# Four pairs of units by seven block products in each feed-forward phase instead of three

## The chip, the core and the metric

One NeuronCore of a Trainium2 chip runs the whole program. The metric is the device time in microseconds of one execution, from the runs of the same program.

## What is computed

A trunk of four layers over 256 tokens of width 1024. Each layer is a feed-forward block, an attention block (stick-breaking, differential, forgetting or again stick-breaking) and a second feed-forward block, each added to x, and at the end comes a norm. The change touches the feed-forward blocks alone, of which there are eight:

```python
D, F = 1024, 2816
def swiglu(x, w_gate, w_up, w_down):
    return (jax.nn.silu(x @ w_gate) * (x @ w_up)) @ w_down
...
x = x + 0.5 * swiglu(rms_norm(x, norm_g[i, 0]), ffn_w_gate[i, 0], ffn_w_up[i, 0], ffn_w_down[i, 0])
```

## The kernel before

**Precision.** Every product is made of three: each operand is split into a rounded part (hi, type fp32r) and the rest (lo = value - hi), and `product` adds hi*hi, hi*lo and lo*hi into PSUM. So each weight chunk (1 MB, 128x2048) is loaded into a slot of `raw`, turned into `w_hi` on ScalarE (`hi`, L462) and into `w_lo` on VectorE (`lo`, L750), and only then is it used by TensorE. `w_hi` and `w_lo` are rings of six chunks (`RING`), so chunk c may be split only when chunk c - 6 has been used (`slot_free`).

**Units.** The 2816 columns of gate and up are 11 units of 256 (`UNITS`). A plain unit has two chunks, `top` and `bottom` (the two halves of the contraction, gate and up side by side), each multiplied with both blocks of 128 tokens; that is 4 x 12 = 48 matmuls of 512 columns. Then silu and the product with up (`silu` on ScalarE, `gated` on VectorE), four transposes on TensorE (`hidden`), a split of the result (`hidden_hi`, `hidden_lo`) and the unit's `down` chunk, 24 matmuls into the four accumulating banks `acc`.

**Pairs.** Two neighbouring units can be made together by a scheme of seven block products instead of eight (token block by half of the contraction, on one side; half of the contraction by unit, on the other). The four weight blocks are b11, b12, b21, b22; VectorE forms four sums of them (`form`: t1, t2, t3, t4, each 128x2048), of which b12 itself isn't used. The seven parts used by TensorE are b11, t1, t2, b21, t3, t4, b22 (`PARTS`), each a split chunk of its own and a `quarter` of 12 matmuls. The results in PSUM are put together by copies on ScalarE (`copied`), sums on VectorE (`summed`), `pair_silu` and `hidden_of`. The sums of the tokens that the scheme needs are made once in each phase (`token_sums_hi`, `token_sums_lo`). `SEVEN` = 2, 5, 8 are the units at which a pair begins; units 0, 1, 4, 7, 10 are plain. So a phase has 5 x 2 + 3 x 7 + 11 = 42 split chunks and 33 loads.

**Order.** All orders are written by hand. `FFN_ORDER` sets the order of the chunks, which ScalarE and VectorE walk with `split_to(c)` (split all up to chunk c, in order), with the other work put between. `plan` gives each load a slot and the event that frees it: four slots of `raw` in turn, and two of `extra`, one for the result of t1 and t4 (`SUMS`), one for b22 (`EXTRA`). The SyncE queue issues the loads in order, each behind the wait for its slot. The engines run their lists in order and meet at semaphores; TensorE waits for `lo_ready` before each chunk, VectorE for `hi_ready`, ScalarE for the load or the form, and for the ring.

In the trace L1259, L1260 and L1261 are the three matmuls of `product`; L1461 is `hidden` (4 transposes), L1417 `pair_hidden` (8 for a pair); L750 the split on VectorE, L763, L766, L770, L774 the forms t1, t3, t2, t4; L814 `hidden_lo`, L844 `token_sums_lo`, L903 `summed`, L848 `gated`, L854 and L918 the products with up in a pair; on ScalarE L462 is the split, L485 `hidden_hi`, L530 `copied`, L496, L534 and L548 the silus; L1172 is the update of x that ends a phase.

## Time and profile before

| | us |
|---|---|
| median of 3 runs (1890.7 to 1891.03) | 1890.84 |
| the profiled execution, its own time | 1890.51 |
| its span | 1888.3 |
| busy in the span: TensorE | 1874.2 (99%) |
| VectorE | 1532.0 (81%) |
| ScalarE | 1073.1 (57%) |

The span is what the profiler records between the first and the last instruction; 2.2 us lie around it. The busy time of TensorE counts each matmul to its modelled end, so that neighbours overlap: what counts is the distance from one start to the next. The busy time of a VectorE instruction is likewise a little longer than the distance to the next one.

### The profile page before, as it was taken

The numbers are of one execution on the slowest core, as the hardware profiler recorded it, in microseconds if no ns is written. First come the engines' busy times: TensorE is split into PE (matmuls) and PEld (weight loads), VectorE is DVE, ScalarE is ACT, GpSimd is POOL, SyncE is SP. The second block draws the span as 40 slices with busy tenths as digits, with TensorE's granted clock in tenths as the row PEclk, the third lists the DMA queues.
The fourth block names the chain that finished last, engine by engine and source line by source line (L and its number), as shares of the span: only waits on it lengthen the run. The fifth ranks groups of instructions, "written<-read, shape, count | busy, mean of one in ns | idle before, by whom it ended". The sixth has DMA issues, their size and how long they took to land.

```text
span 1888.3 us, 22487 instructions
## 1 busy us (share of the span) xinstructions
PE 1874.2 (99%) x9380; PEld 1586.9 (84%) x9380; DVE 1532.0 (81%) x1312; ACT 1073.1 (57%) x1107; POOL 19.9 (1%) x34
## 2 busy tenths in 40 slices
PE   9999999999999999999999999999999999999998
PEld 7888998888888898788888889988888888998886
DVE  7987568987898778898789875689879987559985
ACT  6655555655565544565566554466555654556653
POOL 0000000000000000100000000000000000000000
PEclk9999999999999999999999999999999999999999
DMA  6556343446254642454625454435463544533552
GB/s 249 201 231 267 135 157 134 201 201 244 94 226 198 240 159 109 156 201 200 256 103 226 197 221 157 175 116 201 200 267 122 227 196 191 183 130 137 228 196 86
DMA packets 50052, 350.13 MB, mean 185 GB/s; under 512 B 6168, under 2 KB 6432, under 8 KB 7968
## 3 DMA queue, kind: packets, MB, share of 16 engines
q1 hardware_dynamic: 49360, 346.54, 47.6%
q10 hardware_dynamic: 592, 2.17, 0.3%
q8 instruction: 74, 1.21, 0.3%
q14 instruction: 26, 0.21, 0.0%
HBM read 347.63 MB, written 1.06 MB: 185 GB/s over the span
## 4 chain that ended last, share of the span: by engine, by line
PE 89%; DVE 7%; ACT 2%; issue 1%; DMA 0%; POOL 0%; POOLq 0%; ACTq 0%; DVEq 0%
PE work L1259 18%; PE work L1261 18%; PE work L1260 18%; PE acc L1259 10%; PE acc L1261 10%; PE acc L1260 10%; DVE w_lo L750 3%; PE work L1417 1%; PE acc L1303 1%; PE work L1461 1%; PE work L1586 1%; ACT w_hi L462 1%; PE work L1552 0%; DMA x<-x_dram 0%; PE work L1556 0%
## 5 line engine op out<-in xcount | busy, mean ns | idle before, releaser
L750 DVE TENSOR_TENSOR w_lo<-raw,w_hi 128x2048 fp32r<-128x2048 f32 x327 | 741.3, 2283 | 33.6 <-ACT w_hi L462 33.5
L462 ACT ACTIVATE w_hi<-raw 128x2048 fp32r<-128x2048 f32 x327 | 613.9, 1909 | 83.3 <-DVE raw L770 63.2
L1259 PE MATMUL work<-w_hi,xg 128*128 128x512 f32 x1040 | 411.2, 395 | 1.0 <-DVE xg L1184 1.0
L1261 PE MATMUL work<-w_hi,xg 128*128 128x512 f32 x1040 | 405.6, 390 | 0.0
L1260 PE MATMUL work<-w_lo,xg 128*128 128x512 f32 x1040 | 404.9, 389 | 0.0
L1259 PE MATMUL acc<-w_hi,m_hi 128*128 128x512 f32 x824 | 325.6, 395 | 0.2
L1261 PE MATMUL acc<-w_hi,m_lo 128*128 128x512 f32 x824 | 321.2, 390 | 0.0
L1260 PE MATMUL acc<-w_lo,m_hi 128*128 128x512 f32 x824 | 320.9, 389 | 0.0
L1261 PEld LDWEIGHTS work<-w_hi,xg 128*128 128x128 f32 x1040 | 195.3, 188 | 41.5
L1259 PEld LDWEIGHTS work<-w_hi,xg 128*128 128x128 f32 x1040 | 195.3, 188 | 39.5 <-issue 1.2
L1260 PEld LDWEIGHTS work<-w_lo,xg 128*128 128x128 f32 x1040 | 195.5, 188 | 38.3
L1261 PEld LDWEIGHTS acc<-w_hi,m_lo 128*128 128x128 f32 x824 | 154.7, 188 | 32.7
L1259 PEld LDWEIGHTS acc<-w_hi,m_hi 128*128 128x128 f32 x824 | 154.8, 188 | 31.7 <-DVE w_lo L750 1.0
L1260 PEld LDWEIGHTS acc<-w_lo,m_hi 128*128 128x128 f32 x824 | 154.9, 188 | 30.7
L750 DVE TENSOR_TENSOR w_lo<-extra,w_hi 128x2048 fp32r<-128x2048 f32 x72 | 164.2, 2280 | 0.0
L462 ACT ACTIVATE w_hi<-extra 128x2048 fp32r<-128x2048 f32 x72 | 135.3, 1913 | 45.8 <-DVE extra L763 36.6
L1261 PE MATMUL work<-w_hi,wide_r 128*128 128x512 f32 x384 | 149.8, 390 | 0.0
L1259 PE MATMUL work<-xg,w_hi 128*128 128x256 f32 x512 | 148.7, 290 | 0.6 <-DVE fg L963 0.5
L1261 PE MATMUL work<-xg,w_lo 128*128 128x256 f32 x512 | 144.7, 283 | 0.0
L1260 PE MATMUL work<-xg,w_hi 128*128 128x256 f32 x512 | 144.7, 283 | 0.0
L485 ACT ACTIVATE m_hi<-work 128x512 fp32r<-128x512 f32 x88 | 49.9, 595 | 136.5 <-PE work L1417 109.8
L814 DVE TENSOR_TENSOR m_lo<-work,m_hi 128x512 fp32r<-128x512 f32 x88 | 58.3, 684 | 67.5 <-ACT m_hi L485 67.5
(199 smaller groups left out, 2175.4 us busy)
## 6 DMA issues: line engine op xcount, KB each, us to landing
raw<-stream_dram SPq DMA_DIRECT2D x303, 1024.0 KB, 5.0
extra<-stream_dram SPq DMA_DIRECT2D x24, 1024.0 KB, 6.9
x<-x_dram SPq DMA_DIRECT2D x2, 512.0 KB, 7.9
raw<-stream_dram ACTq DMA_DIRECT2D x2, 512.0 KB, 7.5
scratch<-cum_rows ACTq DMA_DIRECT2D x1, 1024.0 KB, 6.6
cst<-consts_dram SPq DMA_DIRECT2D x1, 832.0 KB, 6.4
out_dram<-x SPq DMA_DIRECT2D x3, 256.0 KB, 2.4
final_gain<-final_gain_dram SPq DMA_DIRECT2D x1, 512.0 KB, 6.7
```

Of the source, the lines that this page charges most:

```text
L462: nc.scalar.activation(w_hi[:, c % RING, :], raw_at(place), ACT.Copy).then_inc(hi_ready, 1)
L485: nc.scalar.activation(m_hi[:, u % 2 * 2:u % 2 * 2 + 2, :], halves(hidden_bank(s)), ACT.Copy).then_inc(h_hi_ready, 1)
L750: nc.vector.tensor_tensor(w_lo[:, c % RING, :], raw_at(place), w_hi[:, c % RING, :].bitcast(F32), ALU.subtract).then_inc(lo_ready, 1)
L814: nc.vector.tensor_tensor(m_lo[:, u % 2 * 2:u % 2 * 2 + 2, :], halves(hidden_bank(s)), m_hi[:, u % 2 * 2:u % 2 * 2 + 2, :].bitcast(F32), A ...
L1259: nc.tensor.matmul(dst, a_hi, b_hi, start=start, stop=False, skip_group_check=skip)
L1260: nc.tensor.matmul(dst, a_hi, b_lo, start=False, stop=False, skip_group_check=skip)
L1261: return nc.tensor.matmul(dst, a_lo, b_hi, start=False, stop=stop, skip_group_check=skip)
L1303: ins = nc.tensor.transpose(turned(bank)[:, d, :], x_part(bank)[:, d * P:(d + 1) * P], ident)
L1417: ins = nc.tensor.transpose(hidden_bank(s)[:, t * T + tb * P:t * T + (tb + 1) * P], h[:, t * P:(t + 1) * P], ident)
L1461: ins = nc.tensor.transpose(hidden_bank(s)[:, t * T + tb * P:t * T + (tb + 1) * P], hidden_source(s)[tb][:, t * P:(t + 1) * P], ident)
L1586: nc.tensor.matmul(bank, v[:, 0, cols], w[:, 0:T], start=True, stop=True)
```

## The change

- `SEVEN` = 3, 5, 7, 9: four pairs. Plain are units 0, 1, 2. The three plain units come first, then the four pairs one behind the other; before, plain units and pairs took turns. A phase has 3 x 2 + 4 x 7 + 11 = 45 split chunks, still 33 loads.
- The forms are made in place: t1 in the slot of b12, t2 over t1, t3 over b11, t4 over b21. So the two slots of `extra` become slots for loads, for the four blocks of a pair and for what is loaded between pairs (`plan`).
- The parts of a pair have three orders: `FIRST_PAIR` for unit 3, `NEXT_PAIR` for 5 and 7, `LAST_PAIR` for 9, with the `down` of earlier units between them. The end of a pair (last silu, last product with up, transposes) lies within the next one.
- The PSUM banks that the pairs use change from pair to pair (`ROLES`), and the intermediate tiles too (`pair_tiles`, a new tile `odd_parts`).
- VectorE splits one chunk of the next phase less ahead of the phase's end. `DMA_SCRATCH` goes from 8192 to 2048.

```diff
 UNITS = FF // COLS
-SEVEN = 2, 5, 8
+SEVEN = 3, 5, 7, 9
...
 RAW = 4
-DMA_SCRATCH = 8192
+ROLES = {s: ((3, 2, 1, 0), (1, 0, 3, 2))[i % 2] for i, s in enumerate(SEVEN)}
+DMA_SCRATCH = 2048
 RING = 6
...
-FORMS = "t1", "t3", "t2", "t4"
+FORMS = "t1", "t2", "t3", "t4"
 PARTS = "b11", "t1", "t2", "b21", "t3", "t4", "b22"
-PAIR_ORDER = *PARTS[:5], "down", *PARTS[5:]
+FIRST_PAIR = "b11", "t1", "t2", "b21", "t3", "b22", "down", "t4"
+NEXT_PAIR = "b11", "t1", "t2", "t3", "b22", "b21", "down", "down_next", "t4"
+LAST_PAIR = "b11", "t1", "t2", "t3", "b21", "down", "t4", "b22"
...
 def ffn_order():
     order = []
-    for s in range(UNITS):
-        if s in SEVEN:
-            order += [(what, s - (what == "down")) for what in PAIR_ORDER]
-        elif s - 1 in SEVEN:
-            continue
-        elif s - 2 in SEVEN:
-            order += [("top", s), ("bottom", s), ("down", s - 2), ("down", s - 1)]
-        else:
-            order += [("top", s), ("bottom", s)] + [("down", s - 1)] * (s > 0)
-    return order + [("down", UNITS - 1)]
+    for s in PLAIN:
+        order += [("top", s), ("bottom", s)] + [("down", s - 1)] * (s > 0)
+    downs = PLAIN[-1]
+    for s in SEVEN:
+        for what in pair_order(s):
+            if what in PARTS:
+                order.append((what, s))
+            else:
+                order.append(("down", downs))
+                downs += 1
+    return order + [("down", s) for s in range(downs, UNITS)]
...
-SUMS, EXTRA = RAW, RAW + 1
+SLOTS = RAW + 2
...
+
+    def load(what, layer, n, j, slots, until, release):
+        place = min(slots, key=lambda i: freed[i][0])
+        filled[place] += 1
+        loads.append((what, layer, n % 3, j, place, freed[place][1]))
+        freed[place] = until, release
+        return place, filled[place]
...
+        if not att:
+            freed[RAW:] = [(c0 + 2, ("top", no * len(PLAIN) + 1))] * 2
...
-                uses.append((what, no, j, *places["b12"]))
+            if what == "b11":
+                c = {part: c0 + order.index((part, j)) for part in PARTS}
+                last_form = len(FORMS) * (no * len(SEVEN) + SEVEN.index(j) + 1)
+                homes = {part: load(part, layer, n, j, range(SLOTS), until, release) for part, until, release in (
+                    ("b11", c["t3"], ("lo", c["t3"] + 1)), ("b12", c["b21"] + 1.5, ("form", last_form)),
+                    ("b22", c["b22"], ("lo", c["b22"] + 1)), ("b21", c["t4"], ("lo", c["t4"] + 1)))}
+            if what in PARTS:
+                home = homes[{"t1": "b12", "t2": "b12", "t3": "b11", "t4": "b21"}.get(what, what)]
...
-                              ("lo", c0 + order.index(("b22", SEVEN[earlier])) + 1)))
+                mixed = not att and ("b11", SEVEN[0]) in order[:w - c0] and j < SEVEN[-1]
+                home = load(what, layer, n, j, range(SLOTS if mixed else RAW), w, ("lo", w + 1))
...
-                    copied(1, 1, first_part)
+                    def last_silu(s):
+                        act.wait_ge(part_psum, len(PARTS) * (f * len(SEVEN) + SEVEN.index(s)) + part_number(s, "t4"))
+                        nc.scalar.activation(pair_tiles(SEVEN.index(s))[3], work[:, ROLES[s][0], 0:COLS], ACT.Silu,
+                                             scale=r_col[:, 1:2]).then_inc(pair_silu_ready, 1)
+
...
+                    split_to(q + 2)
+                    last_silu(SEVEN[SEVEN.index(s) - 1])
+                    split_to(q + 3)
+                    copied(1, u_bank, first_part)
+                    split_to(q + (5 if s < SEVEN[-1] else 4))
+                    copied(3, u_bank, first_sum)
+                    hidden_hi(s - 2)
                     hidden_hi(s - 1)
-                    split_to(q + 5)
...
+                    copied(2, w_bank, second_part)
+                    if s < SEVEN[-1]:
+                        split_to(q + 7)
+                        pair_silu(2, second_part, 1)
+                        pair_silu(3, first_sum, 0)
+                        split_to(q + 8)
+                        pair_silu(1, first_part, 0)
+                        split_to(q + 10)
+                        return
...
+
                 if what == "t1":
-                    if j == SEVEN[0]:
-                        dve.wait_ge(top_used, no * len(PLAIN) + 1)
-                    dve.wait_ge(raw_loaded[place["t3"]], 16 * USES[q + PAIR_ORDER.index("t3")][4])
-                    ins = nc.vector.tensor_tensor(raw_at(SUMS), b12, b11, ALU.subtract)
+                    loaded("b11")
+                    loaded("t1")
+                    ins = nc.vector.tensor_tensor(t1, t1, b11, ALU.subtract)
+                elif what == "t2":
+                    loaded("b22")
+                    dve.wait_ge(lo_ready, at["t1"] + 1)
+                    ins = nc.vector.tensor_tensor(t1, b22, t1, ALU.subtract)
...
-                    ins = nc.vector.tensor_tensor(b11, b12, b11, ALU.add)
+                    dve.wait_ge(form_ready, formed)
+                    dve.wait_ge(lo_ready, at["b11"] + 1)
+                    ins = nc.vector.tensor_tensor(b11, t1, b11, ALU.subtract)
...
-                    ins = nc.vector.tensor_tensor(raw_at(SUMS), b21, b11, ALU.subtract)
+                    dve.wait_ge(form_ready, formed)
+                    dve.wait_ge(lo_ready, at["b21"] + 1)
+                    ins = nc.vector.tensor_tensor(b21, b21, t1, ALU.subtract)
...
                         hidden_lo(0)
                         token_sums_lo((2,))
+                        split_to(c0 + 7)
+                        gated(1, 0)
+                        gated(1, 1)
+                        q = c0 + FFN_ORDER.index(("b11", s + 2))
                         form("t1", q)
-                    else:
-                        form("t1", q)
-                        split_to(q)
+                        split_to(q + 1)
+                        form("t2", q)
+                        form("t3", q)
+                        return
+                    q = c0 + FFN_ORDER.index(("b11", s + 1))
+                    hidden_lo(1)
+                    split_to(q + 2)
+                    gated(s, 0)
+                    split_to(q + 3)
+                    gated(s, 1)
+                    form("t4", q)
+                    split_to(q + 4)
+
...
+                        return
+                    if s > SEVEN[1]:
+                        form("t3", q)
+                    split_to(q + 2)
+                    last_hidden(SEVEN[SEVEN.index(s) - 1])
+                    if s < SEVEN[-1]:
+                        split_to(q + 5)
                         hidden_lo(s - 2)
                         hidden_lo(s - 1)
-                    form("t3", q)
-                    form("t2", q)
-                    gated(s, 0)
-                    gated(s, 1)
+                        form("t4", q)
+                        summed(2, second_part, "t3", u_bank)
+                        split_to(q + 6)
+                        hidden_of(s, 2, second_part, 1)
+                        summed(3, first_sum, "b22", w_bank)
+                        split_to(q + 7)
+                        hidden_of(s, 3, first_sum, 0)
+                        summed(1, first_part, "b21", z_bank)
+                        form("t1", q + 9)
+                        split_to(q + 8)
+                        hidden_of(s, 1, first_part, 0)
+                        split_to(q + 10)
+                        form("t2", q + 9)
+                        return
...
-                split_to(c0 + FFN_CHUNKS + 2)
+                split_to(c0 + FFN_CHUNKS + 1)
...
-                    quarter(1, block_of(1, 1), q + 6, False, True)
+                    quarter(u_bank, sum_of(S2), at("t2"), False, False)
                     if s == SEVEN[0]:
+                        quarter(z_bank, block_of(0, 1), at("b21"), True, True)
+                        pe.wait_ge(part_copied, 3 * p + 2)
+                        quarter(u_bank, sum_of(S3), at("t3"), False, False)
+                        pe.wait_ge(part_copied, 3 * p + 3)
                         pe.wait_ge(token_lo_ready, BANKS * (f + 1))
-                    quarter(3, sum_of(S4), q + 7, False, True)
+                        quarter(w_bank, sum_of(S4), at("b22"), False, True)
+                        unit_down(s - 1).then_inc(down_used, 1)
+                    else:
+                        pair_hidden(p - 1, s - 2)
+                        pair_hidden(p - 1, s - 1)
+                        pe.wait_ge(part_copied, 3 * p + 2)
+                        quarter(u_bank, sum_of(S3), at("t3"), False, False)
+                        if s < SEVEN[-1]:
+                            pe.wait_ge(part_copied, 3 * p + 3)
+                            quarter(w_bank, sum_of(S4), at("b22"), False, True)
+                        pe.wait_ge(h_split, f * UNITS + s - 1)
+                        quarter(z_bank, block_of(0, 1), at("b21"), True, True)
+                        unit_down(s - 2).then_inc(down_used, 1)
+                        if s < SEVEN[-1]:
+                            unit_down(s - 1).then_inc(down_used, 1)
+                    pe.wait_ge(pair_sums_ready, 3 * p + sum_number(s, 2))
+                    quarter(u_bank, block_of(1, 1), at("t4"), False, True)
```

On VectorE, before: from the first form of the pair of units 5 and 6 to its fourth form.

```order
L763 TENSOR_TENSOR extra<-raw 128x2048
L750 TENSOR_TENSOR w_lo<-raw,w_hi 128x2048
L814 TENSOR_TENSOR m_lo<-work,m_hi 128x512 x2
L766 TENSOR_TENSOR raw<-extra,raw 128x2048
L770 TENSOR_TENSOR raw<-raw 128x2048
L848 SCALAR_TENSOR_TENSOR scratch<-work,r_col,scratch 128x256 x2
L750 TENSOR_TENSOR w_lo<-extra,w_hi 128x2048
L750 TENSOR_TENSOR w_lo<-raw,w_hi 128x2048 x3
L814 TENSOR_TENSOR m_lo<-work,m_hi 128x512
L774 TENSOR_TENSOR extra<-raw 128x2048
```

The same engine now: from the first form of the pair of units 7 and 8 (L832 is t1, L836 t2, L840 t3, L844 t4, L815 the split, L975 the last product with up of the pair before, L884 `hidden_lo`) up to its fourth.

```order
L832 TENSOR_TENSOR extra<-extra,raw 128x2048
L815 TENSOR_TENSOR w_lo<-raw,w_hi 128x2048
L924 SCALAR_TENSOR_TENSOR scratch<-scratch,r_col 128x256
L815 TENSOR_TENSOR w_lo<-raw,w_hi 128x2048
L815 TENSOR_TENSOR w_lo<-extra,w_hi 128x2048
L836 TENSOR_TENSOR extra<-raw,extra 128x2048
L840 TENSOR_TENSOR raw<-extra,raw 128x2048
L815 TENSOR_TENSOR w_lo<-extra,w_hi 128x2048
L975 SCALAR_TENSOR_TENSOR odd_parts<-work,r_col,odd_parts 128x256
L815 TENSOR_TENSOR w_lo<-raw,w_hi 128x2048 x2
L815 TENSOR_TENSOR w_lo<-extra,w_hi 128x2048
L884 TENSOR_TENSOR m_lo<-work,m_hi 128x512 x2
```

The forms t2 and t3 now stand ahead of the split of t2 and behind those of the next b11 and t1, and no plain unit stands between two pairs.

On ScalarE, before: from the last split ahead of a pair's first copy out of PSUM (L530), past its `hidden_hi` (L485), to its last silu (L548).

```order
L462 ACTIVATE w_hi<-raw 128x2048 x3
L530 ACTIVATE scratch<-work 128x512
L485 ACTIVATE m_hi<-work 128x512
L462 ACTIVATE w_hi<-raw 128x2048
L530 ACTIVATE scratch<-work 128x512 x2
L462 ACTIVATE w_hi<-extra 128x2048 x2
L534 ACTIVATE scratch<-scratch,r_col 128x256
L462 ACTIVATE w_hi<-raw 128x2048 x2
L534 ACTIVATE scratch<-scratch,r_col 128x256
L462 ACTIVATE w_hi<-raw 128x2048
L548 ACTIVATE pair_h<-work,r_col 128x256
```

The same engine now, in the pair of units 5 and 6, from the split of t2 (L493 is the split, L572 the last silu of the pair of unit 3, L563 the copies, L516 `hidden_hi`).

```order
L493 ACTIVATE w_hi<-extra 128x2048
L572 ACTIVATE pair_h<-work,r_col 128x256
L493 ACTIVATE w_hi<-raw 128x2048
L563 ACTIVATE scratch<-work 128x512
L493 ACTIVATE w_hi<-extra 128x2048
L493 ACTIVATE w_hi<-raw 128x2048
L563 ACTIVATE odd_parts<-work 128x512
L516 ACTIVATE m_hi<-work 128x512 x2
L563 ACTIVATE odd_parts<-work 128x512
```

The splits of t3 and of b22 now stand behind a silu and a copy that wait for TensorE, t4 of the pair before and b11 of this one.

## Rows read from the trace of the kernel before

**Rows 1.** The page's first part: busy us (share of the span) and instructions of each engine.
```profile
PE 1874.2 (99%) x9380; PEld 1586.9 (84%) x9380; DVE 1532.0 (81%) x1312; ACT 1073.1 (57%) x1107; POOL 19.9 (1%) x34
```
**Rows 2.** The waits: engine line waited for: us in total, times, longest.
```profile
PE work L1259 <- DVE w_lo L750: 2.0, 2, 1.3
DVE w_lo L750 <- ACT w_hi L462: 33.5, 33, 1.8
ACT w_hi L462 <- DMA raw<-stream_dram: 20.0, 34, 4.1
```
**Rows 3.** Windows: one whole phase, then one pair and plain unit; length, each engine busy (instructions), clock, DMA share, GB/s.
```profile
1233.79:1411.95 178.16, 178.16 (x815) 147.47 (x814) 155.71 (x119) 107.90 (x102) 1.06 (x2) 1.00 0.52 202
1299.41:1347.06 47.65, 47.65 (x218) 39.52 (x217) 43.04 (x30) 27.72 (x24) 0.00 (x0) 1.00 0.54 218
```
**Rows 4.** TensorE's timeline (start us, us, line, out<-in): two matmuls, twelve apart.
```profile
1289.19 0.39 PE L1259 MATMUL work<-w_hi,wide_r 128*128 128x512 f32 x1
...
1291.91 0.39 PE L1259 MATMUL work<-w_hi,xg 128*128 128x512 f32 x1
```
**Rows 5.** The timeline of TensorE around a single unit's transposes, ahead of unit 1's bottom chunk.
```profile
1255.59 0.60 PE L1461 MATMUL work<-cst,scratch 128*128 128x128 f32 x4
1255.94 0.48 PE L1259 MATMUL work<-w_hi,xg 128*128 128x512 f32 x1
1256.26 0.39 PE L1260 MATMUL work<-w_lo,xg 128*128 128x512 f32 x1
```
**Rows 6.** VectorE's timeline from the first form of a phase on.
```profile
1258.70 2.28 DVE L763 TENSOR_TENSOR extra<-raw 128x2048 f32<-128x2048 f32 x1
1260.90 2.28 DVE L766 TENSOR_TENSOR raw<-extra,raw 128x2048 f32<-128x2048 f32 x1
1263.21 2.29 DVE L770 TENSOR_TENSOR raw<-raw 128x2048 f32<-128x2048 f32 x1
...
1268.41 6.69 DVE L750 TENSOR_TENSOR w_lo<-raw,w_hi 128x2048 fp32r<-128x2048 f32 x3
1275.02 2.28 DVE L774 TENSOR_TENSOR extra<-raw 128x2048 f32<-128x2048 f32 x1
...
1280.62 0.68 DVE L903 TENSOR_TENSOR scratch<-work,scratch 128x512 f32<-128x512 f32 x1
1281.22 2.28 DVE L750 TENSOR_TENSOR w_lo<-extra,w_hi 128x2048 fp32r<-128x2048 f32 x1
1283.42 0.47 DVE L854 SCALAR_TENSOR_TENSOR scratch<-scratch,r_col 128x256 f32<-128x256 f32 x1
1283.82 0.68 DVE L903 TENSOR_TENSOR scratch<-work,scratch 128x512 f32<-128x512 f32 x1
```
**Rows 7.** ScalarE's timeline in the same phase: splits, then a copy that waits for TensorE.
```profile
1307.45 5.53 ACT L462 ACTIVATE w_hi<-raw 128x2048 fp32r<-128x2048 f32 x3 [3.06 <-DVE raw L770]
1317.52 0.60 ACT L530 ACTIVATE scratch<-work 128x512 f32<-128x512 f32 x1 [4.55 <-PE work L1261]
```
**Rows 8.** Timelines of the first phase: a form, a split, and TensorE around it.
```profile
34.27 2.28 DVE L763 TENSOR_TENSOR extra<-raw 128x2048 f32<-128x2048 f32 x1
41.79 2.28 DVE L750 TENSOR_TENSOR w_lo<-extra,w_hi 128x2048 fp32r<-128x2048 f32 x1
...
29.56 0.40 PE L1260 MATMUL work<-w_lo,xg 128*128 128x512 f32 x1
...
44.22 0.47 PE L1259 MATMUL work<-w_hi,scratch_r 128*128 128x512 f32 x1 [0.63 <-DVE w_lo L750]
44.52 0.40 PE L1260 MATMUL work<-w_lo,scratch_r 128*128 128x512 f32 x1
```
**Rows 9.** VectorE's timeline: the updates that end the first phase and the one of rows 6.
```profile
186.67 0.69 DVE L1172 SCALAR_TENSOR_TENSOR x<-acc,x 128x512 f32<-128x512 f32 x1 [2.11 <-PE acc L1261]
...
1411.95 0.69 DVE L1172 SCALAR_TENSOR_TENSOR x<-acc,x 128x512 f32<-128x512 f32 x1 [2.12 <-PE acc L1261]
```
**Rows 10.** Windows of 5 us, columns as in rows 3: the busiest of DMA.
```profile
1280.00:1285.00 5.00, 5.00 (x24) 4.14 (x23) 5.00 (x7) 3.59 (x4) 0.00 (x0) 1.00 1.00 421
```

More of the change, by code:

```diff
@@ L119, in phases @@
     return out
-SUMS, EXTRA = RAW, RAW + 1
+SLOTS = RAW + 2
 def plan():
-    uses, loads, users, places = [], [], [], {}
+    uses, loads = [], []
+    freed, filled = [(-1, None)] * SLOTS, [0] * SLOTS
+    def load(what, layer, n, j, slots, until, release):
[4 more added lines that the diff above has]
+        return place, filled[place]
     for layer, n, c0, att, no in phases():
@@ L144, in plan @@
-            for load in ("b12",) if what == "t1" else () if what in FORMS or what == "b22" else (what,):
-                r = len(users)
-                places[load] = r % RAW, r // RAW + 1
-                loads.append((load, layer, n % 3, j, r % RAW, users[r - RAW] if r >= RAW else None))
-                users.append(("form", len(FORMS) * (p + 1)) if load in ("b11", "b21") else
-                             ("lo", c0 + order.index(("t3", j)) + 1) if load == "b12" else ("lo", w + 1))
-            if what == "t1":
-                earlier = SEVEN.index(j) - 1
-                loads.append(("b22", layer, n % 3, j, EXTRA,
-                              ("top", no * len(PLAIN) + 1) if earlier < 0 else
-                              ("lo", c0 + order.index(("b22", SEVEN[earlier])) + 1)))
+            if what == "b11":
[4 more added lines that the diff above has]
+                    ("b22", c["b22"], ("lo", c["b22"] + 1)), ("b21", c["t4"], ("lo", c["t4"] + 1)))}
@@ L357, in hidden_bank @@
         def hidden_bank(s):
[L358 removed]
+            if s in PLAIN:
+                return work[:, (0, 2, 0)[s], :]
+            if s == SEVEN[-1]:
+                return work[:, ROLES[s][2], :]
+            if s == UNITS - 1:
+                return work[:, ROLES[SEVEN[-1]][0], :]
+            return work[:, ROLES[s][0] if s in SEVEN else ROLES[s - 1][1], :]
         def hidden_source(s):
@@ L892, in plain_step @@
+                        hidden_of(s, 3, first_sum, 0)
+                        summed(1, first_part, "b21", z_bank)
+                        form("t1", q + 9)
+                        split_to(q + 8)
+                        hidden_of(s, 1, first_part, 0)
+                        split_to(q + 10)
+                        form("t2", q + 9)
+                        return
                     split_to(q + 4)
-                    if s > 1:
-                        hidden_lo(s)
+                    hidden_lo(s - 2)
@@ L895, in plain_step @@
+                    hidden_lo(s - 1)
                     form("t4", q)
-                def pair_step(s):
-                    p, q = f * len(SEVEN) + SEVEN.index(s), c0 + FFN_ORDER.index(("b11", s))
-                    def summed(i, place, part, bank):
-                        dve.wait_ge(part_copied, 3 * p + i)
-                        dve.wait_ge(part_psum, len(PARTS) * p + part)
-                        nc.vector.tensor_tensor(place, work[:, bank, :], place, ALU.add).then_inc(pair_sums_ready, 1)
-                    if s == SEVEN[0]:
-                        hidden_lo(s - 1)
@@ L925, in ffn @@
+                    last_hidden(s)
+                    summed(3, first_sum, "b22", w_bank)
+                    hidden_of(s, 3, first_sum, 0)
+                    hidden_lo(s)
+                    split_to(t4 + 4)
+                    hidden_lo(s + 1)
                 for s in range(UNITS):
```

206 lines of the change are left out of this document (109 added, 97 removed).

## Prediction

> **What bounds the kernel now.** I read the page's first part, then the waits, then the timelines of one phase. TensorE is busy for 99% of the span, VectorE for 81%, ScalarE for 57% [rows 1]. TensorE waits for a split only twice, 2.0 us in all, both in the first phase [rows 2]. A plain unit with a pair takes 47.65 us [rows 3]: 204 matmuls at a pitch of (1291.91 - 1289.19) / 12 = 0.2267 us [rows 4] are 46.25, the twelve transposes about 1.40. Four transposes cost 1256.26 - 1255.59 - 0.23 = 0.44 us [rows 5], a pair's eight 0.96. So TensorE is dense in the feed-forward blocks, and a matmul taken away there is worth 0.2267 us, as long as VectorE can keep up. That is the question, for in the same stretch VectorE is busy for 43.04 us of 47.65 [rows 3]. The windows also show the granted clock at 1.00 (2.4 GHz) throughout.
>
> **What the change takes from TensorE.** A fourth pair makes 7 quarters of what were 8. One quarter of 12 matmuls goes in each phase: 12 x 0.2267 = 2.72 us, in eight phases 21.8. Transposes and down products stay.
>
> **What it adds on VectorE.** Start to start, a 128x2048 split takes (1275.02 - 1268.41) / 3 = 2.203 us, a form 2.20, and 0.11 more where it waits for the instruction just ahead (1260.90 to 1263.21); a 128x512 sum 0.60, a 128x256 product 0.40 [rows 6]. A phase gains 3 splits, 4 forms, 3 sums and 4 products and loses 4 products: 7 x 2.203 + 1.8 = 17.2 us. VectorE was busy for 155.7 us of 178.2 [rows 3]; 173 us of a phase that ought to shrink to 175.4 leaves nothing for its waits.
> Here first the row says that a 128x2048 instruction takes 2.28 us by itself and 2.203 in a row [rows 6]. The Trainium skill (VectorE: DVE Perf Modes, The TRN2 errata) gives (N + 151)/0.96 ns for an fp32 tensor_tensor, 2.29 us; by that as a pitch the 50 large instructions below would take 4.4 us more in each phase and the kernel some 35 us more. I keep to the row.
>
> **A pair in its steady state.** The order of VectorE in pairs 5 and 7 has 9 splits and 4 forms (28.64 us), 5 instructions of 0.60 (3.0), 4 of 0.40 (1.6) and two forms with 0.11 more: 33.5 us. TensorE needs 132 x 0.2267 + 0.96 = 30.9. Each of these pairs lacks 2.6 us on VectorE, which the lead from the plain units must pay. Before, a pair had a plain unit beside it and 4.6 us to spare.
>
> **The sum of one phase**, from the anchor of [rows 6]. At 1258.70 VectorE has done all ahead of the first form; the same instructions stand ahead of that place after the change, where the split of unit 2's bottom chunk comes instead. TensorE starts down 0 at 1256.26 + 23 x 0.2267 = 1261.47 [rows 5]. I follow both to the chunk where the backlog is largest, down 7 in the last pair.
> TensorE without a wait: down 0, unit 2 and down 1 are 96 matmuls, pair 3 with down 2 is 108, pairs 5 and 7 are 132 each, and b11, t1, t2, t3 and b21 of pair 9 are 60: 528 x 0.2267 = 119.7. Transposes: 2 x 0.44 + 3 x 0.96 = 3.8. Down 7 could start at 1384.9.
> VectorE: 34 splits and 16 forms are 50 x 2.203 = 110.2; 8 `hidden_lo`, one token sum and 9 `summed` are 18 x 0.60 = 10.8; 16 products 6.3; six forms that wait for their predecessor 0.7. That is 128.0, and ends at 1386.7. To this come waits that I find by walking through the lists: 0.3 us at the split of down 1 (ScalarE has a silu ahead of it that waits for half of unit 1), 0.2 at b22 of pair 3 (the ring: down 1 must be used), 0.3 at down 2 (ScalarE behind the copy of b11), and 0.6 each at t3 and b22 of pair 5 (ScalarE behind the last silu of pair 3 and the copy of b11). Together 2.0, so 1388.7. Its last instruction ends 0.08 later, TensorE starts 0.15 after that (44.07 to 44.22) and its first pitch is 0.08 longer [rows 8]: 1389.0. TensorE is late by 4.1 us, spread over t2 or t3 and the first down of each pair.
> From down 7 on TensorE needs the same as without a wait, since VectorE's remaining work up to the phase's end, some 20 us, fits beside 24 of TensorE. The phase becomes 4.1 - 2.7 = **1.3 us longer**. VectorE's idle 2.12 us before the update [rows 9] was its reserve at the end and can't be used in the pairs.
>
> **The first phase.** VectorE stands at the same place at 34.27, TensorE's down 0 starts at 29.56 + 23 x 0.2267 = 34.77 [rows 8]. The lead is 0.50 instead of 2.77, so VectorE is 2.27 later, but the waits of 2.0 fall away: late by 4.3. In return the first phase already lost 1.4 us before (34.77 to 186.67 is 151.9 us, 1261.47 to 1411.95 is 150.5 [rows 8, 9]), by the forms in front of t1; unit 2 now stands there. Net 4.3 - 2.7 - 1.4 = +0.2.
> **Sum**: 7 x 1.33 + 0.2 = +9.5 us on 1890.5, the profiled execution's own time, which is 0.3 under the median: **1900.0**.
>
> **What I cost at nothing.** ScalarE: it has 9 x 1.81 (5.53 for three [rows 7]) and some 5 us of small work in a pair, 21 of 31; only its order costs, as above. The split of a chunk that VectorE no longer makes ahead of the phase's end falls behind the update; where attention follows, it is needed some 6 us later, and TensorE has two value chunks before it. The loads: SyncE issues them in order, each behind its slot. Four of them leave together early in a phase; at 421 GB/s [rows 10] 1 MB takes 2.5 us, so b12 of pair 3 is there about 4 us and b22 about 10 ahead of its form. Later each slot is freed 8 us or more before the form or split that wants its load. In-place forms wait for the split of what they overwrite; that one stands ahead of them on VectorE anyway, so only the 0.11 is left. If this cover is gone, each microsecond of VectorE idle within the pairs is a microsecond of the phase, eight times.
>
> **Rivals.**
> A. TensorE stays the bound. Each phase gets its 2.72 us and the first its 1.4: 1890.5 - 21.8 - 1.4 = 1867. For it: 99% against 81% busy [rows 1]. Against it: the pair's ledger, 33.5 against 30.9; it would need 4 us more lead at the anchor, or splits 4% faster. The Trainium skill (Perfetto Trace Analysis, Identifying the Most-Contended Engine) has the engine with the highest occupancy optimized first; that speaks for A, and the trace contradicts it in the window of a pair.
> B. The waits on VectorE don't arise, because ScalarE gets its work off earlier than I walk it. Then a phase is late by 2.1 and gains 0.7: 7 x 0.7 less, 1886. It decides between gain and loss at 2.7 us of lateness a phase.
> C. VectorE finds more waits. Now it has idle gaps of up to 1.8 us behind ScalarE's splits [rows 2], and ScalarE waits 4.55 us for a part at one copy [rows 7]. In the changed order splits of t3 and b22 stand behind such a copy in each pair. One more microsecond in each of three pairs, eight times: 1924; half of that 1912.
> D. The change doesn't do what it says, that is, the matmuls don't go: then lateness alone, over 1920. The list of matmuls speaks against it.
>
> **Numbers.** The forecast, 1893 to 1906: 0.52. C, 1906 to 1930: 0.22, of which two thirds lie under 1914. B and what lies between it and the forecast, 1884 to 1893: 0.16. A: 0.07. D and worse: 0.03. The range 1884 to 1914 holds 0.52 + 0.16 + 0.15. The bounds of my unknown cost, the waits, are 0 and 5 us a phase, which it takes in up to about 3.7. A measurement tells some 0.2%, 3.8 us, from no change: faster (under 1887) is A and a third of B, 0.13; same 0.17; slower 0.70.
>
> **What would show it.** Right: the waits list TensorE behind the split on VectorE at 3 or 4 places a phase, 0.5 to 1.5 us each, in pairs 7 and 9 and not in pair 3; VectorE has hardly an idle gap from unit 1 to down 7 and is busy for about 170 of 179.5 us; phases end 179.5 us apart; ScalarE's copies and the loads don't appear as releasers of TensorE. Wrong: TensorE dense at 175.4 us a phase (A), or VectorE with gaps behind ScalarE in every pair (C).

## The result, and the profile after

The changed kernel takes **1900.44 us** (median; 1900.38 to 1900.58) against 1890.93 us of the kernel before on the same chip: a ratio of 1.0051, 95% interval 1.0039 to 1.0063. The forecast was 1900.0. The profiled executions have spans of 1898.5 and 1888.3 us, 10.2 us apart, both at a granted clock of 0.999.

The page's first and fourth parts of the changed kernel, to be read against [rows 1]: busy us (share) and instructions of each engine, then who holds the chain that ended last.
```profile
PE 1864.2 (98%) x9284; PEld 1566.8 (83%) x9284; DVE 1670.9 (88%) x1392; ACT 1131.6 (60%) x1155; POOL 30.9 (2%) x34
...
PE 55%; DVE 34%; issue 5%; ACT 4%; DMA 0%; POOL 0%; POOLq 0%; DVEq 0%; ACTq 0%
```
The fourth part of the page of the kernel before:
```profile
PE 89%; DVE 7%; ACT 2%; issue 1%; DMA 0%; POOL 0%; POOLq 0%; ACTq 0%; DVEq 0%
```
The 96 matmuls are gone (9380 to 9284), VectorE has 139 us more to do, that is 17.4 a phase, and it now holds 34% of the chain, where it held 7%. TensorE's matmuls are still "busy" for 98%, and by that share alone it would be the bound. Two other rows of the page speak against that: its weight loads take 83%, less than VectorE's 88%, and the chain.

The waits (engine line waited for: us in total, times, longest), beside [rows 2], where TensorE had two:
```profile
DVE w_lo L815 <- ACT w_hi L493: 30.5, 41, 1.8
...
PE work L1371 <- ACT scratch L563: 12.4, 22, 1.5
...
PE acc L1371 <- DVE w_lo L815: 9.1, 16, 0.7
```
21.5 us of waits in 38 places. The two releasers are VectorE's split and ScalarE's copy of a quarter's result.

The window of the whole phase, beside the first line of [rows 3]:
```profile
1238.93:1418.60 179.67, 177.00 (x803) 144.95 (x802) 171.01 (x129) 113.72 (x108) 1.06 (x2) 1.00 0.49 189
```
It is 1.51 us longer with 12 matmuls fewer, and VectorE is busy for 171.0 of 179.7 us. TensorE's timeline marks four waits in it (start, us, line, in brackets the idle time ahead and its releaser). A fifth place, at 1354.58, is late without a mark:
```profile
1350.49 0.50 PE L1371 MATMUL work<-w_hi,scratch_r 128*128 128x512 f32 x1 [0.15 <-ACT scratch L563]
...
1354.58 0.50 PE L1371 MATMUL work<-w_hi,wide_r 128*128 128x512 f32 x1
...
1363.45 0.50 PE L1371 MATMUL acc<-w_hi,m_hi 128*128 128x512 f32 x1 [0.42 <-DVE w_lo L815]
...
1382.40 0.39 PE L1373 MATMUL work<-w_hi,wide_r 128*128 128x512 f32 x1
1384.00 0.50 PE L1371 MATMUL work<-w_hi,scratch_r 128*128 128x512 f32 x1 [1.21 <-ACT scratch L563]
1384.34 0.40 PE L1372 MATMUL work<-w_lo,scratch_r 128*128 128x512 f32 x1
...
1394.16 0.50 PE L1371 MATMUL acc<-w_hi,m_hi 128*128 128x512 f32 x1 [0.74 <-DVE w_lo L815]
```
They are t2, t3 (the unmarked one) and the first down of pair 7, then t2 and down 7 of pair 9. Pairs 3 and 5 have none. A wait costs more than its bracket says: from 1382.40 to 1384.00 it is 1.60 us where the pitch is 0.23, that is 1.37 for a bracket of 1.21, and the pitch behind it is 0.34, another 0.11. With such additions, and with some 0.4 us at 1354.58, the brackets' 2.5 us become the 3.9 that the first experiment finds.

VectorE's timeline of that phase: the split that now stands at the anchor of the prediction's ledger, the waits, the run up to the split of down 7, and its idle time behind that.
```profile
1263.83 2.28 DVE L815 TENSOR_TENSOR w_lo<-raw,w_hi 128x2048 fp32r<-128x2048 f32 x1
...
1266.43 2.29 DVE L815 TENSOR_TENSOR w_lo<-raw,w_hi 128x2048 fp32r<-128x2048 f32 x1 [0.32 <-ACT w_hi L493]
...
1316.36 2.29 DVE L815 TENSOR_TENSOR w_lo<-raw,w_hi 128x2048 fp32r<-128x2048 f32 x1 [0.47 <-ACT w_hi L493]
1319.20 2.29 DVE L815 TENSOR_TENSOR w_lo<-extra,w_hi 128x2048 fp32r<-128x2048 f32 x1 [0.55 <-ACT w_hi L493]
...
1381.43 2.28 DVE L815 TENSOR_TENSOR w_lo<-raw,w_hi 128x2048 fp32r<-128x2048 f32 x1
...
1391.83 2.28 DVE L815 TENSOR_TENSOR w_lo<-raw,w_hi 128x2048 fp32r<-128x2048 f32 x1
...
1405.46 0.69 DVE L970 TENSOR_TENSOR odd_parts<-work,odd_parts 128x512 f32<-128x512 f32 x1 [1.81 <-PE work L1373]
```
From 1321 us to the split of down 7 at 1391.83 the timeline marks no gap. That split ends at 1391.83 + 2.28 = 1394.11, and TensorE starts on it at 1394.16. Before the change, gaps of 0.4 to 2.5 us stood all through the pairs; now, from the anchor on, VectorE's first gap of more than 0.6 us comes after TensorE has taken the last late chunk, where it is of no use.

### The profile page after: what moved, and what is told of

It is laid out like the page before. It is cut to its first block, busy times and chain, and to the rows that moved or that the text cites. A ratio compares the mean times of both kernels' runs of the same rounds, so it can differ in the third digit from the quotient of the medians.

```text
span 1898.5 us, 22591 instructions
## 1 busy us (share of the span) xinstructions
PE 1864.2 (98%) x9284; PEld 1566.8 (83%) x9284; DVE 1670.9 (88%) x1392; ACT 1131.6 (60%) x1155; POOL 30.9 (2%) x34
## 3 DMA queue, kind: packets, MB, share of 16 engines
q8 instruction: 74, 1.21, 0.3%
## 4 chain that ended last, share of the span: by engine, by line
PE 55%; DVE 34%; issue 5%; ACT 4%; DMA 0%; POOL 0%; POOLq 0%; DVEq 0%; ACTq 0%
DVE w_lo L815 18%; PE work L1371 11%; PE work L1373 11%; PE work L1372 11%; PE acc L1371 6%; PE acc L1373 6%; PE acc L1372 6%; ACT w_hi L493 3%; DVE raw L840 2%; DVE extra L844 2%; DVE extra L832 1%; DVE extra L836 1%; DVE m_lo L884 1%; DVE scratch L970 1%; PE acc L1415 1%
## 5 line engine op out<-in xcount | busy, mean ns | idle before, releaser
L815 DVE TENSOR_TENSOR w_lo<-raw,w_hi 128x2048 fp32r<-128x2048 f32 x311 | 706.3, 2284 | 28.6 <-ACT w_hi L493 27.2
L493 ACT ACTIVATE w_hi<-raw 128x2048 fp32r<-128x2048 f32 x311 | 588.2, 1914 | 94.2 <-DVE raw L836 60.1
L1371 PE MATMUL work<-w_hi,xg 128*128 128x512 f32 x880 | 347.4, 395 | 1.0 <-DVE xg L1296 1.0
L1373 PE MATMUL work<-w_hi,xg 128*128 128x512 f32 x880 | 343.0, 390 | 0.0
L1372 PE MATMUL work<-w_lo,xg 128*128 128x512 f32 x880 | 342.6, 389 | 0.0
L493 ACT ACTIVATE w_hi<-extra 128x2048 fp32r<-128x2048 f32 x112 | 214.1, 1911 | 113.6 <-DVE extra L836 80.5
L815 DVE TENSOR_TENSOR w_lo<-extra,w_hi 128x2048 fp32r<-128x2048 f32 x112 | 255.0, 2282 | 3.3 <-ACT w_hi L493 3.3
L1373 PE MATMUL work<-w_hi,wide_r 128*128 128x512 f32 x512 | 199.7, 390 | 0.0
L1373 PEld LDWEIGHTS work<-w_hi,xg 128*128 128x128 f32 x880 | 165.2, 188 | 35.1
L1371 PEld LDWEIGHTS work<-w_hi,xg 128*128 128x128 f32 x880 | 165.3, 188 | 33.9 <-issue 1.2
L1372 PEld LDWEIGHTS work<-w_lo,xg 128*128 128x128 f32 x880 | 165.4, 188 | 32.7
L1371 PE MATMUL work<-w_hi,scratch_r 128*128 128x512 f32 x256 | 102.3, 400 | 11.3 <-ACT scratch L563 11.3
L1373 PEld LDWEIGHTS work<-w_hi,wide_r 128*128 128x128 f32 x512 | 96.1, 188 | 20.6
```

The costliest lines, as they stand in the source:

```text
L493: nc.scalar.activation(w_hi[:, c % RING, :], raw_at(place), ACT.Copy).then_inc(hi_ready, 1)
L815: nc.vector.tensor_tensor(w_lo[:, c % RING, :], raw_at(place), w_hi[:, c % RING, :].bitcast(F32), ALU.subtract).then_inc(lo_ready, 1)
L1371: nc.tensor.matmul(dst, a_hi, b_hi, start=start, stop=False, skip_group_check=skip)
L1372: nc.tensor.matmul(dst, a_hi, b_lo, start=False, stop=False, skip_group_check=skip)
L1373: return nc.tensor.matmul(dst, a_lo, b_hi, start=False, stop=stop, skip_group_check=skip)
```

## The experiments

In what follows, V is the theory that VectorE's sum up to down 7, waits included, sets the end of every phase; S is that something else does (ScalarE's order, TensorE itself). All ratios are to the kernel before, on the same chip, with 95% intervals.

**Take VectorE's work away.** Every form on half of its columns; the sums of the other half are left out:
```
-ins = nc.vector.tensor_tensor(t1, t1, b11, ALU.subtract)
+ins = nc.vector.tensor_tensor(t1[:, 0:HALF], t1[:, 0:HALF], b11[:, 0:HALF], ALU.subtract)
```
and so for t2, t3 and t4.

> The changed kernel with each of the four forms of every pair made on the first 1024 of its 2048 columns only (the sums are wrong in the other half), so that VectorE has 16 x 1.07 = 17 us less to do in a phase and all else stays. Theory V (the pairs are bound by VectorE's throughput): its lateness of about 4 us a phase goes, TensorE becomes dense, phases of 175.4 us, 1866 us. Rival S (the stalls come from where ScalarE makes its copies, or from waits in the pairs): most of the stalls stay, 1885 us or more.

Measured: 1867.97 us (1867.85 to 1868.07), ratio 0.9879 (0.9864 to 0.9893). The windows of the same phase:
```profile
1218.55:1394.36 175.81, 175.81 (x803) 145.21 (x802) 155.42 (x128) 114.39 (x108) 1.06 (x2) 1.00 0.51 193
```
TensorE is dense (175.81 busy of 175.81) with ScalarE's work and all orders unchanged. So 175.8 is what TensorE needs for this phase, where the prediction had 175.4, and 179.67 - 175.81 = 3.9 us of it are lateness. Without the lateness the changed kernel would be 22.9 us faster than the one before (1890.87 to 1867.97); VectorE's lateness costs 1900.44 - 1867.97 = 32.5.

**Add work on VectorE, in the changed kernel and in the one before.** One split of each phase, that of t4 in pair 5, is made twice:
```
 dve.wait_ge(hi_ready, c + 1)
+if USES[c][0] == "t4" and USES[c][2] == SEVEN[1]:
+    done(nc.vector.tensor_tensor(w_lo[:, c % RING, :], raw_at(place),
+                                 w_hi[:, c % RING, :].bitcast(F32), ALU.subtract))
 nc.vector.tensor_tensor(w_lo[:, c % RING, :], raw_at(place), w_hi[:, c % RING, :].bitcast(F32),
                         ALU.subtract).then_inc(lo_ready, 1)
```

> The changed kernel with one VectorE instruction more in each phase: the split of the chunk t4 of the pair of units 5 and 6 is made twice (same values, 2.31 us with its wait). Theory V: VectorE has no slack from there to down 7 of the last pair, so all of it shows, 8 x 2.31 = +18.5 us, 1919 us. Rival S: VectorE has slack and it is hidden at least in part, below 1910 us.

> The kernel before with the same addition, the split of t4 of the pair of units 5 and 6 made twice in each phase. Theory V: there a pair with its plain unit leaves VectorE 4.6 us, so the 2.31 us vanish, 1891 us, no change. If VectorE were as tight before, it would be 1909 us.

Measured: in the changed kernel 1918.83 us (1918.74 to 1919.55), ratio 1.0148 (1.0133 to 1.0164), which is +18.4 where eight times 2.31 is 18.5. In the kernel before 1890.79 us, ratio 1.0 (0.999 to 1.0009). The same instruction at the same place costs all of itself after the change and nothing before it. In the kernel before, it goes into the gaps behind it: that of 0.43 us at 1337.56 and that of 1.16 at 1348.99 are gone and one of 1.89 is 1.33. VectorE's timeline of the kernel before, then with the addition:
```profile
1348.99 1.29 DVE L814 TENSOR_TENSOR m_lo<-work,m_hi 128x512 fp32r<-128x512 f32 x2 [1.16 <-ACT m_hi L485]
...
1366.29 0.69 DVE L814 TENSOR_TENSOR m_lo<-work,m_hi 128x512 fp32r<-128x512 f32 x1 [1.89 <-ACT m_hi L485]
```
```profile
1366.58 0.69 DVE L817 TENSOR_TENSOR m_lo<-work,m_hi 128x512 fp32r<-128x512 f32 x1 [1.33 <-ACT m_hi L485]
```

**VectorE's waits in pair 5.** ScalarE has the last silu of pair 3 and the copy of b11 ahead of the high halves of t3 and b22; both are put one split later, and on VectorE the last product too:
```
-split_to(q + 2)
+split_to(q + (3 if s == SEVEN[1] else 2))
 last_silu(SEVEN[SEVEN.index(s) - 1])
-split_to(q + 3)
+split_to(q + (4 if s == SEVEN[1] else 3))
 copied(1, u_bank, first_part)
```

> The changed kernel; in the pair of units 5 and 6 alone, ScalarE makes the split of t3 ahead of the last silu of the pair before and the split of b22 ahead of the copy of b11, and VectorE its split of t3 ahead of the last product of the pair before. Same work, only the order. Theory V: VectorE's two waits there, 0.47 and 0.55 us, go in the six phases that have them, and each microsecond saved on VectorE before down 7 comes back: -6 us, 1894 us. Rival (such waits are covered, the bound lies elsewhere): 1900 us.

Measured: 1899.16 us (1898.84 to 1899.43), ratio 1.0044 (1.0029 to 1.0059). Both waits went, but the six phases that had them are only 0.22 to 0.31 us shorter (from a phase's first update to the next one's) for 1.02 of waits, and the first phase is 0.24 longer. The expectation was missed. VectorE's timeline in pair 5 shows where the rest went:
```profile
1319.60 2.28 DVE L815 TENSOR_TENSOR w_lo<-raw,w_hi 128x2048 fp32r<-128x2048 f32 x1
1322.71 1.29 DVE L884 TENSOR_TENSOR m_lo<-work,m_hi 128x512 fp32r<-128x512 f32 x2 [0.83 <-ACT m_hi L516]
```
A new wait of 0.83 us at `hidden_lo` of pair 5. It subtracts what ScalarE copies out of TensorE's transposes, and TensorE, which is not late in pair 5, makes those in its own time. Whatever lead VectorE has there is capped by TensorE.

**Does the cap hold it?** The form t4, which needs nothing from TensorE, goes ahead of that wait:
```
 split_to(q + 5)
+if s == SEVEN[1]:
+    form("t4", q)
 hidden_lo(s - 2)
 hidden_lo(s - 1)
-form("t4", q)
+if s > SEVEN[1]:
+    form("t4", q)
```

> As e4_pair5_order, and in pair 5 VectorE makes the form t4 (2.2 us) ahead of the two small differences for the hidden values, at which it waited 0.83 us a phase in e4. Nothing is left out and nothing added; only VectorE's order in pair 5 changes. Theory V (in e4 the lead of VectorE in pair 5 was capped by this wait for TensorE's transposes): the wait goes, VectorE is 0.7 to 0.8 us earlier at every split behind it, and the phases shorten by as much: about 1893.5 us (1892 to 1895). Rival (the wait was not what held e4, TensorE's lateness comes from pairs 7 and 9 alone): no change from e4, 1899 us.

Measured: 1894.97 us (1894.38 to 1895.7), ratio 1.0021 (1.0012 to 1.0031). The wait is gone: 4.2 us of the expected 5.7, at the edge of what was expected. The six phases are now 0.97 to 1.05 us shorter than in the changed kernel, which is the whole of the two waits, 0.47 + 0.55. The first and the fourth phase don't have them and gain nothing; the expectation had counted eight phases. With e4, V holds: the waits in pair 5, once the third behind them is out of the way too, are worth 1900.4 - 1895.0 = 5.4 us.

**Is ScalarE's copy a cause?** The largest wait of TensorE names ScalarE's copy of b11. In pairs 7 and 9 it is put ahead of the high half of t3:
```
-split_to(q + 3)
+split_to(q + (3 if s == SEVEN[1] else 2))
 copied(1, u_bank, first_part)
```

> The changed kernel with ScalarE's copy of b11 put ahead of the high half of t3 in pairs 7 and 9 (in pair 5 it stays). In the changed kernel TensorE waits at t2 of pair 9 for this copy (1.2 us, ScalarE the releaser). Theory V (the copy comes as late as the split of t2 does, both hang on VectorE's forms and splits): the copy is early now, TensorE waits at the same places for VectorE's split of t2 instead and starts at most 0.15 us earlier, what it gains there it loses at down 7: 1899 to 1900.5 us. Rival S (ScalarE's order of work is a cause of its own): the 1.2 us a phase goes, about 1890 us.

Measured: 1900.41 us (1900.09 to 1901.21), no change from 1900.44. TensorE's timeline at t2 and down 7 of pair 9:
```profile
1383.88 0.47 PE L1371 MATMUL work<-w_hi,scratch_r 128*128 128x512 f32 x1 [1.06 <-DVE w_lo L815]
...
1394.19 0.50 PE L1371 MATMUL acc<-w_hi,m_hi 128*128 128x512 f32 x1 [0.87 <-DVE w_lo L815]
```
It waits at the same place for VectorE's split of t2 instead, starts 0.12 us earlier, and loses that at down 7. In the changed kernel the split of t2 ends at 1381.43 + 2.28 = 1383.71 and the copy some 0.2 us later, because the copy stood behind the high half of t3, for which ScalarE waited for VectorE's form. Both ends hang on VectorE; the profile names the one that came last.

**Move VectorE's work to GpSimd.** The first three products of pairs 5 and 7 are made there:
```
 def hidden_of(s, i, place, tb):
+    if s in SEVEN[1:-1]:
+        return
...
+nc.gpsimd.tensor_scalar(up, up, r_col[:, tb:tb + 1], None, ALU.mult).then_inc(up_scaled, 1)
...
+nc.gpsimd.tensor_tensor(gate, gate, up, ALU.mult).then_inc(pair_h_ready, 1)
```

> The changed kernel with six of the twelve products of a phase (those of the first three values of pairs 5 and 7, 0.40 us each on VectorE) made on GpSimd, in two steps each (up part by the norm's factor, then times the gate part). VectorE loses 6 x 0.40 = 2.4 us a phase, all of it between the split of t4 of pair 5 and that of down 7. Theory V (VectorE's sum over that stretch sets the phase's end): 8 x 2.4 = 19 us less if TensorE is still late by as much, and TensorE was late 3.2 us a phase there: about 1881 us (1879 to 1885). Rival P (VectorE's and GpSimd's operations take time from each other, or GpSimd's products come too late for the transposes): VectorE's splits get longer than 2.28 us beside them, or TensorE waits for GpSimd; 1890 to 1905 us. Rival S (VectorE's sum is not what binds): 1900 us.

Measured: 1900.24 us (1900.1 to 1900.69), ratio 1.005 (1.0035 to 1.0065): nothing of the 19 us. VectorE's timeline, the changed kernel first (three instructions, from 1343.38), then this one (the same three):
```profile
1343.38 2.29 DVE L836 TENSOR_TENSOR extra<-raw,extra 128x2048 f32<-128x2048 f32 x1
1345.71 2.29 DVE L840 TENSOR_TENSOR raw<-extra,raw 128x2048 f32<-128x2048 f32 x1
1347.92 2.28 DVE L815 TENSOR_TENSOR w_lo<-extra,w_hi 128x2048 fp32r<-128x2048 f32 x1
```
```profile
1342.26 2.38 DVE L850 TENSOR_TENSOR extra<-raw,extra 128x2048 f32<-128x2048 f32 x1
1344.67 2.71 DVE L854 TENSOR_TENSOR raw<-extra,raw 128x2048 f32<-128x2048 f32 x1
1347.31 2.28 DVE L829 TENSOR_TENSOR w_lo<-extra,w_hi 128x2048 fp32r<-128x2048 f32 x1
...
1349.90 5.03 DVE L829 TENSOR_TENSOR w_lo<-raw,w_hi 128x2048 fp32r<-128x2048 f32 x2
```
VectorE is ahead by 1.1 us, then its forms take 2.38 and 2.71 us in place of 2.29, and two splits 5.03 in place of 4.48, while GpSimd works (GpSimd's timeline of this kernel):
```profile
1333.33 9.61 POOL L475 TENSOR_SCALAR odd_parts<-odd_parts,r_col 128x256 f32<-128x256 f32 x1
1343.03 2.21 POOL L478 TENSOR_TENSOR odd_parts<-odd_parts 128x256 f32<-128x256 f32 x1
1345.22 5.08 POOL L475 TENSOR_SCALAR scratch<-scratch,r_col 128x256 f32<-128x256 f32 x1
```
In sum VectorE is busy for 1670.6 us with 48 instructions fewer, against 1670.9: what was taken off it came back as longer instructions. This is rival P.

**Is it contention, or were these products free?** The same six products stay on VectorE, on 16 columns of 256:
```
+n_cols = 16 if s in SEVEN[1:-1] else COLS
...
-nc.vector.scalar_tensor_tensor(out=place[:, 0:COLS], in0=place[:, COLS:2 * COLS],
-                               scalar=r_col[:, tb:tb + 1], in1=place[:, 0:COLS], op0=ALU.mult,
+nc.vector.scalar_tensor_tensor(out=place[:, 0:n_cols], in0=place[:, COLS:COLS + n_cols],
+                               scalar=r_col[:, tb:tb + 1], in1=place[:, 0:n_cols], op0=ALU.mult,
```

> The changed kernel with the same six products as in e7_pool_products (pairs 5 and 7) kept on VectorE but made on 16 of their 256 columns, so that the rest of these hidden values is left out; GpSimd has no part in it. By VectorE's rows a column costs 1.04 ns (2.203 us for 2048 columns against 0.60 for 512), so a product falls from 0.40 to about 0.15 us and VectorE's stretch is 6 x 0.25 = 1.5 us shorter a phase. Theory V with contention (in e7 the saved time was real, and was taken back by VectorE's operations that ran longer beside GpSimd's): 1900.4 - 8 x 1.5 = 1888.4 us (1886 to 1891). Rival (these products stand in slack, and e7 gained nothing because they bind nothing): 1899 to 1900.5 us.

Measured: 1888.52 us (1888.19 to 1888.67), ratio 0.9986 (0.9977 to 0.9995), where V with contention said 1888.4. The products do bind. So e7 gained nothing because VectorE's other instructions were longer beside GpSimd's by as much as the products had taken.

**All three together** (e5, e6's copy, the products on GpSimd):

> e5, e6 and e7 together: VectorE's two waits of pair 5 and the one behind them gone, ScalarE's copy early in pairs 7 and 9, six products on GpSimd. Theory V: VectorE has 2.4 us less work and about 1.5 us less waiting in the stretch, which is more than TensorE was late there (3.2 us a phase); what is left is TensorE's own sum with at most 0.5 us of waits a phase: about 1876 us (1873 to 1881), faster than both kernels. Rival P (GpSimd takes time from VectorE): 1885 to 1900. If the gains don't add up because TensorE's transposes hold VectorE back elsewhere: 1881 to 1885.

Measured: 1898.12 us (1897.98 to 1898.35), ratio 1.0039 (1.0024 to 1.0054): worse than e5 alone by 3.2 us. The 1876 was missed because its sum had GpSimd's help as a gain; e7 shows why it is none. That explains 1895, not 1898. VectorE's timeline of this run has splits that are half a microsecond longer, and one of them is the last split ahead of that of down 7, where TensorE's wait is marked with 1.17 us against 0.70 in e5:
```profile
1383.85 2.82 DVE L829 TENSOR_TENSOR w_lo<-extra,w_hi 128x2048 fp32r<-128x2048 f32 x1
```
In e7 this split takes 2.28. GpSimd's products fall beside other VectorE instructions here; that this is the whole 3.2 us is not shown.

**Order VectorE's work by what TensorE needs next.** To e5 is added: the product of pair 7's first value goes behind the split of t2 of pair 9, and the form t4 of pair 9 and the difference of hidden unit 8 behind the split of down 7. On ScalarE the copy of b11 comes ahead of the high half of t3, and that of down 7 ahead of the other copies.
```
 split_to(q + 4)
 hidden_lo(s - 2)
+split_to(q + 5)
 hidden_lo(s - 1)
 form("t4", q)
-split_to(q + 5)
...
-split_to(q + (4 if s == SEVEN[1] else 3))
+split_to(q + (4 if s == SEVEN[1] else 3 if s < SEVEN[-1] else 2))
 copied(1, u_bank, first_part)
-split_to(q + (5 if s < SEVEN[-1] else 4))
+split_to(q + 5)
```

> e5_t4_first, and near pair 9 VectorE's work that is not needed yet goes behind what is: the product of pair 7's first value behind the split of t2 (0.4 us earlier for it), the form t4 of pair 9 and the difference of hidden unit 8 behind the split of down 7 (2.8 us earlier for it); on ScalarE the copy of b11 comes ahead of the high half of t3, that of down 7 ahead of the copies behind t2. Nothing is left out. In e5 TensorE was late 0.22, 1.21 and 0.70 us (plus about 0.17 each) in a phase. Theory V (order on VectorE decides which of TensorE's waits are left, sum to t2 of pair 9 then binds): about 0.3 to 0.4 us goes at t2, 0.9 at down 7, at most 0.4 comes back at t4 of pair 9: 0.9 to 1.2 us a phase, 1895.0 - 8 x 1.05 = about 1886.5 us (1885 to 1889), 0.2% under the kernel before. Rival (the new order makes TensorE wait for t4 of pair 9, or b21, by as much as it gains): 1893 to 1897 us.

Measured: **1887.45 us** (1887.14 to 1887.88), ratio **0.998** (0.9971 to 0.999). It computes all that the changed kernel does, lies within the 1885 to 1889 that were expected, and is faster than both, than the kernel before by 0.2%. TensorE's timeline of the phase has three waits left:
```profile
1355.55 0.51 PE L1382 MATMUL acc<-w_hi,m_hi 128*128 128x512 f32 x1 [0.24 <-DVE w_lo L815]
...
1375.56 0.47 PE L1382 MATMUL work<-w_hi,scratch_r 128*128 128x512 f32 x1 [0.64 <-DVE w_lo L815]
...
1379.62 0.50 PE L1382 MATMUL work<-w_hi,wide_r 128*128 128x512 f32 x1 [0.20 <-ACT odd_parts L563]
```
The one at down 7 is gone, and the last two are now t2 and t3 of pair 9. VectorE has as much work as in the changed kernel (1670.8 us busy). So the 13 us against the changed kernel come from the order on VectorE and ScalarE and the waits that hang on it. 5.4 of them are e5's; how the other 7.5 divide among the moves made here was not measured.

## Why the prediction was right, and where it was not

The forecast was within 0.5 us, and its mechanism held: VectorE's sum up to down 7 sets the end of a phase. Two terms were wrong in size and a third was missing. That they nearly cancel is luck.

**VectorE's added work.** 17.2 us a phase forecast by starts; busy time rose by 139 / 8 = 17.4.

**The ledger to down 7.** It puts TensorE's start there at 1389.0 with VectorE's anchor at 1258.70. After the change the anchor instruction starts at 1263.83, 5.13 later, and TensorE starts at 1394.16, which is 1389.03 on the ledger's clock. This is the step on which the forecast rests, and it held to 0.1 us. The waits on it came at the five places that were named. Beyond the pitch, start to start, they are 0.40, 0.16, 0.22, 0.54 and 0.64 us, together 1.96, where 0.3, 0.2, 0.3, 0.6 and 0.6 were forecast; the timeline marks only three of them with a bracket. The pitch from the row was right and the 2.29 us by the Trainium skill (VectorE: DVE Perf Modes, The TRN2 errata) is the duration of one instruction by itself, which the rows show as 2.28, not the pitch in a row, 2.203: with it the kernel would have been at 1935.

**What TensorE loses and gets.** 2.72 us a phase, 21.8 in all, were forecast, for 12 matmuls less and transposes that "stay". e1 gives the price for each phase, from first update to first update. The six full phases that are alike (all but the first and the fourth):

| us a phase | forecast | measured | mean of six |
|---|---|---|---|
| TensorE's gain, before less e1 | 2.72 | 2.18 to 2.35 | 2.27 |
| lateness, changed less e1 | 4.1 | 3.84 to 4.21 | 3.92 |
| the phase grows by | 1.33 | 1.51 to 1.86 | 1.65 |

So the term "12 x 0.2267" is right for the matmuls and 0.45 us too large for the phase. Part of it lies in the transposes: from a pair's first one to the next matmul it is 0.79 us before the change (1300.08 to 1300.87) and 0.85 in e1 (1301.62 to 1302.47); the rest wasn't traced. The lateness was 0.2 us smaller than forecast, because TensorE by itself comes to down 7 later than the ledger has it: 3.87 us ahead of 1389.03 by e1, that is 1385.2, against 1384.9.

**Seven equal phases.** The fourth phase of the program, which the sum took for a full one, grew by 0.15 us only. Before the change it had a wait of its own at t1 of its first pair (TensorE's timeline of the kernel before; it is the 1.3 us in the first line of [rows 2]):
```profile
800.73 0.47 PE L1259 MATMUL work<-w_hi,scratch_r 128*128 128x512 f32 x1 [1.34 <-DVE w_lo L750]
```
The prediction put both waits of [rows 2] in the first phase. One was in the fourth, which therefore lost time before the change and gets it back as the first phase does: in e1 the program is 4.64 us shorter from the end of the third phase to the end of the fourth, 2.4 more than in a full phase. The sum should have been 6 x 1.65 + 0.15, with 0.27 for the first phase (forecast 0.2): 10.3 us, and the spans differ by 10.2. The same two errors cancel in rival A's 1867, which e1 meets with 1868.0. The last phase grew most, 1.86; there VectorE's timeline marks 0.46 us of idle time ahead of the form t2 of pair 9 that the others don't have.

**What would show it.** TensorE's waits in pairs 7 and 9 and not in 3: right, at four marked places and one unmarked. Of their sizes, 0.5 to 1.5, two are smaller (0.15 and 0.42). Phases 179.5 apart: 179.7 to 180.1, the fourth 180.8. VectorE busy for 170: 171.0. That ScalarE's copies would not appear as releasers: **wrong**, they are the largest one by total, 12.4 us. The prediction walked VectorE's list only and not TensorE's second condition at t2, the copy of b11. e6 shows that this cost the sum nothing, since that copy's own chain goes back to VectorE's form and ends within 0.2 us of the split.

**Rivals.** A fell with e2, and e1 gives its price. Against A the prediction also said that the trace contradicts it in the window of a pair. It doesn't: in [rows 3] TensorE is busy for all 47.65 us of that window, and only the ledger of the new order spoke against A. B, waits that don't arise: they arose. e4 and e5 took away those of pair 5, 1.0 us by the brackets, and got 1.0 a phase in six phases, 1895.0; the three waits ahead of it, which B's 1886 counts too, were not removed by any run. B left out that VectorE's lead is capped by TensorE's transposes in pair 5, so that the waits' going alone gave next to nothing (e4). D is out by the 96 matmuls that went. C didn't come: in pairs 7 and 9 VectorE's timeline marks no gap up to down 7. "Each microsecond of VectorE idle within the pairs is a microsecond of the phase" holds behind the cap (e2: 18.4 of 18.5; e9: 11.9 of 12) and not ahead of it (e4: 1.3 of 6.4 expected).

## What to carry to other kernels

When a change moves work from a busy engine to one that is nearly as busy, add up both engines' work between the last place where the second one has lead and the chunk where its backlog is largest; the shares over the span (98% against 88% here) didn't tell which of them binds. Count the idle gaps of the second engine by place: those behind the last late chunk, or ahead of a point where it must wait for the first engine anyway, are not to be spent. Then order the lists by what the first engine needs next: with not one instruction less, that was worth 13 us here, more than the change had lost.
